# Block 1 attention by head pairs, with the last subtraction of the gate sigmoid on GpSimd

## The reference

```
def hybrid_layer(x, norm_mix, w_in, w_out_a, w_out_b, w_out_c, w_o, ...):
    proj = rmsnorm(x, norm_mix) @ w_in            # 1024 -> 3*1536 + 3*1024
    q, k, v = heads(proj[..., :3 * MIX_WIDTH])    # 24 heads of 64
    gates = jax.nn.sigmoid(proj[..., 3 * MIX_WIDTH:]).reshape(B, S, 3, D)
    o_a = dilated_mixture(q[:, 0:12], k[:, 0:12], v[:, 0:12])
    o_b = moba_attention(q[:, 12:18], k[:, 12:18], v[:, 12:18])
    o_c = stick_breaking_attention(q[:, 18:24], k[:, 18:24], v[:, 18:24])
    merged = gates[:, :, 0] * (flat(o_a) @ w_out_a) \
           + gates[:, :, 1] * (flat(o_b) @ w_out_b) \
           + gates[:, :, 2] * (flat(o_c) @ w_out_c)
    x = x + merged @ w_o
    ...
```

## Time and profile before

| | |
|---|---|
| median of 3 runs | 1539.34 us (1539.24 to 1539.76) |
| span of the profiled execution | 1537.9 us |
| median less that span | 1.4 us |
| mean granted TensorE clock | 0.994 |
| PE busy | 1484.8 us (97%) |
| DVE busy | 918.7 us (60%) |
| ACT busy | 793.9 us (52%) |
| POOL busy | 91.4 us (6%) |

### The profile page before, as it was taken

How to read it: one execution, slowest core, us unless ns; L and a number is a source line. 1 busy time by engine, 2 the same in 40 slices (tenths; PEclk the granted TensorE clock), 3 DMA queues, 4 the chain that set the end, 5 groups by cost and what they waited for, 6 DMA issues and landing times.

```text
span 1537.9 us, 21514 instructions
## 1 busy us (share of the span) xinstructions
PE 1484.8 (97%) x8288; PEld 1195.1 (78%) x8288; DVE 918.7 (60%) x1687; ACT 793.9 (52%) x1349; POOL 91.4 (6%) x142
## 2 busy tenths in 40 slices
PE   7999998999999999998999999999999899999998
PEld 6887777799887787877789978787776348788776
DVE  4554456766554554455866666677544874669655
ACT  5445786355534445687445554434565302344774
POOL 6050000000000000000000000000000000041220
PEclk9999999999999999999999999999999999999999
DMA  8782334788554754232489654462222001164200
GB/s 275 253 184 83 125 122 164 219 224 215 192 191 164 276 198 155 83 122 98 171 242 261 191 192 165 164 165 68 71 83 74 22 0 39 45 178 134 81 29 29
DMA packets 183701, 220.96 MB, mean 144 GB/s; under 512 B 6619, under 2 KB 103429, under 8 KB 183600
## 3 DMA queue, kind: packets, MB, share of 16 engines
q1 hardware_dynamic: 179376, 211.65, 43.5%
q0 software_dynamic: 3184, 7.93, 2.6%
q10 hardware_dynamic: 1040, 0.00, 0.0%
HBM read 216.55 MB, written 3.01 MB: 143 GB/s over the span
## 4 chain that ended last, share of the span: by engine, by line
PE 78%; DVE 13%; ACT 6%; issue 3%; DMA 0%; DVEq 0%; SPq 0%; ACTq 0%
PE bank L620 21%; PE bank L622 21%; PE bank L621 21%; DVE w_low L1793 2%; PE bank L1107 2%; ACT w_high L1357 1%; PE bank L863 1%; PE bank L1070 1%; PE bank L704 1%; PE bank L807 1%; PE bank L1083 1%; PE bank L838 1%; PE bank L637 1%; PE bank L812 1%; DVE arena L2150 1%
## 5 line engine op out<-in xcount | busy, mean ns | idle before, releaser
L1793 DVE TENSOR_TENSOR w_low<-raw,w_high 128x1024 fp32r<-128x1024 f32 x344 | 414.9, 1213 | 340.8 <-ACT w_high L1357 335.7
L1357 ACT ACTIVATE w_high<-raw 128x1024 fp32r<-128x1024 f32 x352 | 367.0, 1047 | 334.8 <-PE bank L622 284.8
L620 PE MATMUL bank<-w_high,acts_r 128*128 128x512 f32 (+1 forms) x848 | 339.0, 400 | 11.6 <-DVE w_low L1793 4.9
L621 PE MATMUL bank<-w_low,acts_r 128*128 128x512 f32 (+1 forms) x848 | 329.7, 389 | 0.0
L622 PE MATMUL bank<-w_high,acts_r 128*128 128x512 f32 (+1 forms) x848 | 329.7, 389 | 0.0
L620 PE MATMUL bank<-acts_r,w_high 128*128 128x256 f32 (+1 forms) x736 | 228.9, 311 | 1.5 <-DVE arena L2209 1.3
L622 PE MATMUL bank<-acts_r,w_low 128*128 128x256 f32 (+1 forms) x736 | 225.6, 307 | 0.0
L621 PE MATMUL bank<-acts_r,w_high 128*128 128x256 f32 (+1 forms) x736 | 225.6, 307 | 0.0
L620 PEld LDWEIGHTS bank<-w_high,acts_r 128*128 128x128 f32 x848 | 160.2, 189 | 53.5 <-DVE w_low L1793 6.6
L622 PEld LDWEIGHTS bank<-w_high,acts_r 128*128 128x128 f32 x848 | 159.4, 188 | 36.4
L621 PEld LDWEIGHTS bank<-w_low,acts_r 128*128 128x128 f32 x848 | 159.8, 188 | 32.0
(11 more groups left out here) (315 smaller groups left out, 1789.6 us busy)
## 6 DMA issues: line engine op xcount, KB each, us to landing
raw<-in_w_in SPq DMA_DIRECT2D x69, 1024.0 KB, 5.2
raw<-in_w_up SPq DMA_DIRECT2D x64, 512.0 KB, 6.7
raw<-in_w_down SPq DMA_DIRECT2D x32, 1024.0 KB, 4.9
raw<-in_w_ada SPq DMA_DIRECT2D x24, 1024.0 KB, 6.9
raw<-in_w_in SPq DMA_DIRECT2D x34, 512.0 KB, 5.1
raw<-in_w_o SPq DMA_DIRECT2D x8, 1024.0 KB, 7.6
raw<-in_w_out SPq DMA_DIRECT2D x8, 1024.0 KB, 4.9
raw<-in_w_out_c SPq DMA_DIRECT2D x4, 768.0 KB, 5.3
```

The costliest lines, as they stand in the source:

```text
L620: mm(o, lh, rh, start=start, stop=False)
L621: mm(o, lh, rl, start=False, stop=False)
L1357: run(A_(high, src, ACT.Copy), (high_ready, n + 1))
L1793: run(V.tensor_tensor(low, src, high.bitcast(F32), ALU.subtract), split_done(n))
```

## The change

**Units.** 26 units become 10 pair units in a layer (`pairs_of_block1`): A is two results and one tile (4 units), B two heads and both tiles (3), C two heads (3). In step i PE issues `scores(i)`, `second(i-1)`, the filler (8 steps for A of tile 0, 9 for A of tile 1, 10 for B, 9 for C, the rest of 5 at the end), `values(i-1)`. The filler's order is changed so that the first tile of a group ends two steps before the second (`by_tile`).

**PE.** Scores of the two heads alternate between the halves of the rows. For A of tile 1 the third scores of both sides share a bank, so the second of them waits for the first (`third_scored`) and closes the scores. Values have v stationary in 64 columns and the probabilities moving, the two sides in different halves of the columns, and are followed by the spread of the inverse sums. The result has features in partitions; the transposes of `o_tok` are gone.

**ACT and DVE.** ACT copies the transposed probabilities of side 0 (and a third bank for A of tile 1), DVE those of side 1. ACT copies the spread inverse sums, DVE multiplies. `oT` is split in three parts, one for each kind, as soon as the kind is done. For C the relu pass of DVE is gone.

**Gates.** DVE takes the minimum from PSUM (L2076 after), ACT does Abs, Exp, Ln and the last Exp, GpSimd the subtraction.

The diff, cut:

```diff
@@ PE
-                for u in range(len(U) + 2):
+                steps_of = {"A": (8, 9), "B": (10,), "C": (9,)}
+                for i in range(len(U) + 1):
...
-                    advance(filler, 1000 if u >= len(U) else 3 if U[u][0] == "A" else 4)
-                    if u >= 2:
-                        values(u - 2)
+                    advance(filler, steps_of[U[i][0]][U[i][2]] if i < len(U) else 1000)
+                    if i:
+                        values(i - 1)
...
+                    if kind == "A":
+                        for b in range(blocks):
+                            g, jt = b // (t + 1), b % (t + 1)
+                            for side in range(2):
+                                mm(half[side][:, 0:P], v(g * N_A + 2 * p + side, jt), PT[side][:, b * P:(b + 1) * P],
+                                   start=b == 0, stop=b == blocks - 1)
...
-                for u in range(len(U)):
-                    pe.wait_ge(*emptied("o", l, u))
-                for b in range(4):
-                    o = open_bank("oT", l, b)
...
@@ ACT
+                for i in range(len(U) + 1):
+                    if i >= 2:
+                        take_sums(i - 2)
+                    if i:
+                        take_second(i - 1)
+                    if i < len(U):
+                        exponents_of(i)
+                        splits.due("s", l, i, 1)
+                    while len(done) < len(logged):
                         gate_exp_step()
+                    if i in (6, 9):
+                        take_heads_high((6, 9).index(i))
+                    for key in ended_in[(l, i)]:
+                        gate_log_steps(key)
...
@@ DVE
+                    if i:
+                        invert_sums(i - 1)
+                    early = i >= 2 and U[i - 2][0] == "A"
+                    if early:
+                        take_values(i - 2)
+                    if i < len(U):
+                        maximum(i)
+                    if i >= 2 and not early:
+                        take_values(i - 2)
+                    if i:
+                        take_second(i - 1)
...
+                    if i < len(U):
+                        splits.due("s", l, i, 1)
+                        stick_sums(i)
+                    for key in ended_in[(l, i)]:
+                        gate_floor(key)
...
@@ POOL
+            for l in range(LAYERS):
+                for n in range(6 * TILES):
+                    g = gates[:, n % TILES, n // TILES // 2, n // TILES % 2 * 512:(n // TILES % 2 + 1) * 512]
+                    pool.wait_ge(*gate_logged.at(l, n))
+                    run(G.tensor_tensor(g, g, gate_log[:, n % 2, :], ALU.subtract), gate_exponent.by(l, n))
```

More of the change, by code:

```diff
@@ new lines, in values @@
+                    if kind != "C":
+                        n = 1 if kind == "A" else 2
+                        for tt in range(n):
+                            for side in range(2):
+                                inverse = stat[:, (2 * i + side) % 4, 3, tt:tt + 1].to_broadcast([P, DH])
+                                ins = mm(half[side][:, (n + tt) * P:(n + tt + 1) * P], inverse, ident[:, :], start=True, stop=True)
+                    close_bank(ins, "o", l, i)
+                U = pairs_of_block1()
@@ L881, in _ @@
[L881 to L888 removed]
+                    if i < len(U):
+                        scores(i)
+                    if i:
+                        second(i - 1)
@@ L1470, in gate_log_step @@
                     x = gate_log[:, n % 2, :]
-                    act.wait_ge(*emptied("gate", l, 9 + n // TILES, n % TILES))
+                    run(A_(x, bank(*key)[:, :], ACT.Abs, scale=nstat[:, 2, t:t + 1]), emptied(*key))
+                    run.settle()
                     run(A_(x, x, ACT.Exp, scale=-1.0))
@@ L1509, in _ @@
[L1509 to L1517 removed]
+                    run(A_(logged[n], logged[n], ACT.Exp), gates_ready.by(l, n))
```

502 lines of the change are left out of this document (266 added, 236 removed).

## The result

| | before | change |
|---|---|---|
| median | 1539.76 us | 1548.38 us |
| runs | 5, 1539.24 to 1544.46 us and one of 2929.76 | 5, 1546.31 to 1552.17 us |
| ratio | | 1.0056, 95% interval 1.0039 to 1.0073 |
| span of the profiled execution | 1537.9 us | 1544.4 us (its own time 1546.31) |
| mean granted TensorE clock | 0.994 | 0.988 |

The change is slower, by 0.4 to 0.7%. The forecast was 1505 us and its range ended at 1524, so both the sign and the size were wrong.

A forecast was written before the change was run, and what follows sets the result against it. PE, busy for 97% of the span, was taken as the bound. Its stream of 101.3 us plus waits of 1.9, 2.5, 2 and 6 made 113.7 a stage, saving 35 in two layers: 1505 us, range 1485 to 1524.

The forecast's parts named there:

- points 1 to 4: PE's own work in a layer's stage: paired scores, values, dropped `o_tok` transposes, fewer step borders; 101.3 us without waits.
- Rival C: Scores on the two row halves don't overlap; 7.4 us a layer come back, 1520 us; chance 0.09.
- (a): Start of the stage: PE waits until ACT has emptied banks of v; about 1.9 us.
- (b): Step 5: PE wants a gate group's bank again before ACT has reached its Abs; 2.5 us.
- point 5: ACT's busy time in the stage falls from 98.9 to 85 us, DVE's is some 70; neither bounds on average.
- (c): Third step: third transposes bank still holds values just made, ACT has two gate groups before taking them; 2 us.
- (d): Weight roundings stand behind the pair's exponentials while PE's filler wants them; 0.6 us a pair, 6 us.
- point 8: After the stage: ACT is ready about when PE reaches the products with part C; 0 to 1 us waited.
- point 7: GpSimd's gate subtractions, about 1.3 us each, cost nothing by length; 3 to 4 of twelve meet DVE's low parts.
- Rival B: ACT or the port shared by GpSimd and DVE decides, delaying low parts PE waits for; 1519 us, chance 0.14.
- D: Slower: each step becomes a chain rather than a pipeline, deciding from 13 us a step; 1549 us, chance 0.05.
- Rival A: Everything is covered: PE waits only 2 us, stage 105 us; 1487 us, chance 0.22.

The follow-up runs named there:

- e9: e3 with e4's edit, plus ACT's roundings of weights issued ahead of the pair's exponentials; 1494.93 us, 0.9713 of before.
- e3: e1 with the gates as before: ACT copies the bank, DVE does minimum and subtraction in one, GpSimd idle; 1518.56 us, 0.9859 of before.
- e5: e1 with the gates' subtraction moved from GpSimd to DVE, the minimum left in place; 1539.43 us, 1.0001 of before.
- e12: The change with its own gates and the order edits of e1, e6, e4 and e9 together; 1491.98 us, 0.9694 of before.
- e1: The change with DVE's three operations for `cond` moved ahead of layer 0's attention loop; 1539.97 us, 1.0005 of before.
- e4: e1 with four filler steps issued between the second and third bank of transposes; 1521.87 us, 0.9893 of before.
- e11: e1 with the gates' Exp cut to 8 of 512 columns and their Ln left out (not sigmoids); 1511.94 us, 0.9830 of before.
- e2: The kernel before, old attention, with only the change's gates (minimum on DVE, subtraction on GpSimd); 1537.35 us, 0.9991 of before.
- e6: e1 with DVE taking the gates' minimum before the low parts due at a group's end; 1526.63 us, 0.9914 of before.
- e7: e3 with the gates' minimum and subtraction as two GpSimd operations in place of DVE's combined one; 1517.77 us, 0.9859 of before.
- e10: e9 with the gates' minimum and subtraction on GpSimd in place of DVE; 1498.32 us, 0.9735 of before.

## Why the prediction was wrong

The forecast summed PE's own stream and PE's waits. The first half held, the second did not.

**PE's stream of 101.3 us (points 1 to 4): right.** In e9's second stage PE needs 104.1 us and stands for 2.1 of them, in its first 105.8 and 3.7, all at a clock of 1.00, so its stream is 102.0 to 102.1, 0.7 over the sum. Rival C falls: the scores of two heads do pass in twos. At 137.51, in the change, twelve records of 128 columns on the two halves of the rows take 0.94 us with the tail, and twelve of values on the two halves of the columns 0.88:

```profile
136.49 0.88 PE L896 MATMUL bank<-arena 128*64 128x128 f32 x12
...
137.51 0.94 PE L822 MATMUL bank<-arena 64*128 64x128 f32 x12
```

**The start (a) and the gate bank (b): right**, 1.9 and 2.5 forecast, 1.6 to 1.9 and 2.0 measured; but in layer 1 the start wait lies ahead of the stage and not in it. **ACT (point 5)** has 89 and 80 us of busy time in the two stages for the 85 forecast.

**The third bank (c): 2 forecast, 6.7 measured.** The step that failed is the sentence that ACT has two gate groups ahead of taking the values. It counted the burst and forgot its start. Point 5 had booked DVE's 12 minima as 0.68 us each and asked neither what stands ahead of them on DVE nor who waits for them. The burst began 2.3 us late, and the same happens at both units of kind A, tile 1: two waits of 3.0 to 3.7 us, not one of 2. Without the relay the two are still 4.1 us together (e3): the second unit was forgotten in any case.

**Low parts (d): 6 forecast, 8.2 and 9.9 measured.** The price per pair came from block 2, whose steps hold no gate bursts. Four waits for low parts make 5.2 us by themselves. The stick sums (L856), 3.0 and 4.6 more, were in no term: they stood for 3.9 before, and I let them vanish into the price per pair.

**The clock: nothing forecast, about 4.6 us a layer.** The working knew a drop at the transposes of `o_tok` and took it away with them. That longer waits of PE, 1.7 to 3.7 us, bring three new ones in each stage had no term.

**After the stage (point 8): 0 to 1 us forecast, 10.1 measured in layer 0.** It followed the products of C and never asked what `ada_group` itself needs. L716 needs `cond`, last in DVE's order.

**GpSimd (point 7): right in the result.** 24 subtractions, all alike:

```profile
L2629 POOL TENSOR_TENSOR arena<-arena x24: 1263/1284/1305, 140.7 to 745.8; 128x512 f32<-128x512 f32 x24
```

1.28 us as estimated, and e5 shows that moving them changes nothing. The estimate of meetings with DVE's low parts of weights was three or four in twelve; it is one, the last pair of a layer, where the low part at 253.58 starts while POOL is busy until 253.95 and takes 1.45 us for its usual 1.22. (The low part of a kind's heads at 210.84 meets it too, and takes 0.82 for the 0.68 that it takes in e5, without GpSimd.) By the rule of the Trainium skill (SBUF — State Buffer, "SBUF: two separate sides") the two take turns on a shared port pair, whole instructions at a time. The traces agree, here and in the two longer meetings shown at the end. Rival B had the rule right and the number of meetings wrong.

**The sum.** Layer 1: +0.7 (stream), +4.7 (c), +3.9 (d), +4.6 (clock), -1.9 (a, outside the stage) and -0.5 (b) make 11.5, for the 13.1 by which the stage missed 113.7. Layer 0: +0.7, +4.7, +2.2, +4.6, +10.1 and -0.8 (a, b) make 21.5 for 23.4. So 1.6 and 1.9 us stay unexplained. With +5.5 outside the stages and -0.7 at the start the miss is 41.3 us of span: two stages of 113.7 would have made 1503.1 of before's 1537.9, and the profiled execution spans 1544.4.

**The rivals.** D has the price of the result, 1549 for 1548.38, and something of its mechanism: of the ten steps with scores in the change's layer 0 four take 14.6 to 15.8 us (those that start at 137.5, 163.1, 178.9 and 213.5, each with 3.0 to 4.1 us of waiting), the others 8.3 to 10.9, and D said over 13 decides. What it named as the lateness, roundings behind exponentials, is what e9 took away (15 us). But it put ACT late in every step and missed the relay and the silu; that it has the price of the result is luck. It got a chance of 0.05. Its argument against, that ACT is busy for only 8.5 of 10 us in a step, is the same fault as the forecast's: a share of busy time says nothing about the instruction that PE waits for. Rival A, everything covered, at 1487, is nearly what e12 reaches: the room was real.

**Left open.** "Between" the stages is 3 to 6 us longer in every variant. The traces say where: 1.9 us are the start wait of layer 1, in all kernels with pairs; most of these have 1.7 to 1.8 more in front of the transposes of `merged`, and e1, e4, e5 and e11 have 1.1 for a gate bank. In e2, with the old attention (356.3), it is a wait of 2.1 us for the low part of `oT` and a half-clock stretch. No experiment is made for any of these. The parts of e1's loss by cause overlap: e3, e4, e6 and e11 each return 13 to 28 us, and together no more than 48, since removing one wait also removes the clock's share and makes room for the next.

## What to carry to other kernels

When many small steps are merged into a few large ones, read each engine's order at every wait that PE makes: what stands ahead of the one instruction that PE needs, and what that one waits for. Busy shares of 48 to 65% on ACT and DVE here went with 19 to 29 us of waiting on PE in a stage. Put what releases another engine (a minimum of 0.7 us, a silu of 0.6) ahead of what is merely due (low parts of 3.5 us, a burst of 4), give PE filler ahead of a bank that comes free late, and fill an engine's natural hole with its unurgent work. A relay over one more engine is free while steps are short, and was the largest loss once they were long, so two edits are to be tested apart and together: 0.9991 of before for the one (e2) and 0.9859 for the other (e3) did not tell of 1.0005 for both (e1).

## What the runs showed of the hardware

The granted clock dropped to 0.50 (1.2 GHz) for stretches of 3.4 us, mostly behind PE's longer waits: 3.66 us of standing, PE busy again at 143.13, the drop at 144.3. In e9, where no wait in the stages is over 1.9 us, no such stretch lies in either stage. The length of a wait alone doesn't tell, though: e7 waits 2.4 us in each stage without a drop in either, and e12, whose longest wait is 2.0 us in both layers, has one drop in layer 0, at 175.7, and none in layer 1. The Trainium skill (TensorE: Matmul & The Clock Gate, "The HAM clock gate") tells of the same two levels. What I had not expected is their weight in a stage where PE is busy for four fifths of the time: about 4.6 of the 23.4 us missed in layer 0, and of the 13.1 in layer 1.

The other is GpSimd beside DVE. A 128x512 subtraction on GpSimd took 1263 to 1305 ns in all 24 cases of the change, with DVE's copies and maxima, which read PSUM, running beside it. A low part of DVE, which reads two operands of SBUF, was held up when it started while GpSimd was still in a subtraction. Two such starts, in e11 and in e10:

```profile
240.63 1.90 DVE L1832 TENSOR_TENSOR w_low<-raw,w_high 128x1024 fp32r<-128x1024 f32 x1 [2.16 <-ACT w_high L1394]
```
```profile
215.86 2.23 DVE L1837 TENSOR_TENSOR w_low<-raw,w_high 128x1024 fp32r<-128x1024 f32 x1 [3.95 <-ACT w_high L1396]
```

GpSimd had 0.37, 0.82 and 1.15 us left (the change at 253.58, e11, e10), and the low part took 0.23, 0.68 and 1.00 us over its usual 1.22: what was left, less some 0.15 us.
